# Expert weights in transfers of four tiles with 64 KB rows and of two tiles with 32 KB rows

## Chip, cores and metric

The kernel runs on 1 core of one Trainium2 chip. The metric is the device time of one execution in microseconds (us); lower is better. All numbers are fp32 in memory.

## The reference

Three blocks follow each other on 512 tokens of width 1024. The change touches the last part of the first block, an expert-choice feed-forward layer with 16 experts; each expert picks 64 tokens:

```python
def expert_choice_ffn(h, w_router, w_gate, w_up, w_down):
    Bn, N, D = h.shape                                   # 1, 512, 1024
    cap = max(1, CAPACITY_FACTOR * N // N_EXPERTS)       # 64
    logits = jnp.einsum('bnd,de->bne', h, w_router, preferred_element_type=jnp.float32)
    aff = jax.nn.softmax(logits, axis=-1)
    top_w, top_idx = lax.top_k(jnp.swapaxes(aff, 1, 2), cap)
    xe = jax.vmap(lambda hb, ib: hb[ib])(h, top_idx)
    g = jnp.einsum('becd,edf->becf', xe, w_gate)         # 1024 -> 2048
    u = jnp.einsum('becd,edf->becf', xe, w_up)
    y = jnp.einsum('becf,efd->becd', jax.nn.silu(g) * u, w_down)
    y = y * top_w[..., None].astype(y.dtype)
    return jax.vmap(lambda ib, yb: jnp.zeros((N, D), yb.dtype).at[ib.reshape(-1)].add(yb.reshape(-1, D)))(top_idx, y)
```

Its weights are 16 x 3 x 1024 x 2048 numbers, 403 MB, each used once.

## The kernel before

**Weights as tiles.** All matrices of weights are cut into tiles of 128 partitions x 4096 numbers (16 KB per partition, 2 MB). `Core.tiles` lists them in the order of their use; the expert weights are 192 of them, 12 for each expert: two of gate and two of up for the first half of the 2048 hidden channels, the same for the second half, then four of down. In DRAM the tensor `in_w_exp` holds them as 192 blocks of [128 partitions, 4096], laid out by the host (`expert_tiles`), so a row of one transfer is 16 KB long on both sides.

**Places.** A tile lands in a place in SBUF. The ring has four places (`SLOTS`). In the expert stage four of the seven slabs, buffers of 128 x 4224 numbers for activations that are free there, are four more places (`MORE_SLOTS` = slabs 6, 4, 5, 1). `lay_slots` (L289) gives each tile its place: the first 96 expert tiles (`WIDE_RING`, 8 experts) go round all eight places, the other 96 round the four of the ring. `self.before` remembers the tile that had the place last. Slab 3 holds, in the expert stage, the gathered tokens `xe`, the hidden values `hT` and the results `y`; slab 3 also serves the router for its squares.

**Order of the transfers.** SyncE (SP) issues all weight transfers in the order of the tiles, in `issue_weights` (L314). Before each it waits until TensorE has used the tile that was in the place:

```python
engine.wait_ge(self.weight_used.sem, self.before[n] + 1)
to = self.ring_tile(n)[:, 0:kc, 0:cw] if kc <= KC else self.deep_tile(n, kc)
engine.dma_start(to, src).then_inc(self.weight_in[self.slot[n]].sem, 16)
```

TensorE waits for the landing of each tile with `weight_ready` and raises `weight_used` by one after its last matmul on it. Before the stage, `expert_weights` (a function of the stage for gates, projections and output) issues eight expert tiles ahead: two when the layer `pa` has used its last tile, more after `pb`, the last after `wo`.

**TensorE in the expert stage** (`experts`). Two experts are a pair; expert e has tiles 12e to 12e + 11. A tile is 16 matmuls of 512 columns (`two_halves`, L2335). Between them stand, for even experts after their fourth tile, the combine of the pair before (`combine`, L2325, 16 matmuls), for odd ones at the same place the gather of the next pair's tokens (`gather`, L2264, 64 matmuls), and for all the transposes of the hidden values (`turn`, L2362) and, once per pair, those of the one-hot weights (`turn_onehot`, L2273). The last 8 tiles, numbers 184 to 191, are the down weights of experts 14 and 15 by columns (`last_narrow`, L2290), so that the combine of the last pair (L2303) and the sums for the norm that follows (L2314) stand between them. ScalarE and VectorE move the PSUM results on. After the stage, the next weights (`in_w_in` of the second block) take the places of the ring as they come free.

Of the kernel before, what the change touches and what calls it, by code (L numbers as in the profile page):

```python
# [21 lines left out]
P = 128  # L22
D = 1024
KC = D // P
SEQ = 512
# [3 lines left out]
SLOTS = 4  # L29
SLOT_COLS = 512  # L30
BANKS = 8
EXPERTS, CAP, DFF = 16, 64, 2048
EXPERT_TILES = 12
MORE_SLOTS, WIDE_RING = (6, 4, 5, 1), 8 * EXPERT_TILES
LB = 64
NBLK = 9
WIDE = NBLK * LB
# [3 lines left out]
def common_constants():  # L41

    p = np.arange(P)
    ident = np.eye(P)
    ones = np.ones((P, P))
    head = (p[:, None] // 64 == p[None] // 64)
    four = np.arange(4)[None]
    return [("ident", ident), ("ones", ones), ("head", head),
            ("eye64", p[:, None] % 64 == p[None, :64]), ("first32", p[:, None] % 32 == 0), ("pick16", p[:, None] % 32 == np.arange(16)[None]), ("pick4", p[:, None] == 32 * four),
            ("halves32", p[:, None] // 64 == p[None, :32] // 16), ("pick8", p[:, None] == 16 * p[None, :8])]  # L50
# [114 lines left out]
class Core:  # L165


    def __init__(self, nc, ctx, dram):
        self.nc, self.dram = nc, dram
        sb = lambda name, shape, dt=F32: ctx.enter_context(nc.sbuf_tensor(name, shape, dt))  # L170
        self.ring = [sb(f"ring{i}", [P, KC, SLOT_COLS]) for i in range(SLOTS)]
        self.slab_cols = KC * TOK2
        self.slabs = sb("slabs", [P, 7 * self.slab_cols])
        self.slab = [self.slabs[:, i * self.slab_cols:(i + 1) * self.slab_cols] for i in range(7)]
# [15 lines left out]
        def count(name):  # L190
            s = Count(ctx.enter_context(nc.semaphore(name)))
            self.counts.append(s)
            return s
# [25 lines left out]
        turn = [count(f"of_this_stage{i}") for i in range(37)]  # L219
# [6 lines left out]
                            "plain_read", "held", "rows", "step", "ada", "scaled"))  # L226
        self.deep = named(("product", "first", "second", "third", "fourth", "sums", "read", "step"), 20)

        self.weight_in = [count(f"weight_in_slot{i}") for i in range(SLOTS)] + turn[37 - len(MORE_SLOTS):]
        self.ring += [self.slab[i][:, 0:KC * SLOT_COLS].rearrange("p (k c) -> p k c", k=KC) for i in MORE_SLOTS]  # L230
        self.weight_used = count("weight_used")
        self.tiles, self.named, self.issued, self.done = [], {}, 0, 0
        self.dense = set()
# [50 lines left out]
    def plan_laid_out(self, name, w, i):  # L284

        self.named[name] = [(0, SLOT_COLS, [(len(self.tiles), 0, KC, SLOT_COLS)])]
        self.tiles.append((w[i].rearrange("p (k c) -> p k c", k=KC), KC, SLOT_COLS))

    def lay_slots(self, expert_tiles):  # L289

        slots, first = SLOTS + len(MORE_SLOTS), expert_tiles[0]
        freed = [*range(SLOTS, slots), *((first + i) % (SLOTS - 1) for i in range(SLOTS - 1)), SLOTS - 1]
        self.slot, self.turn, self.before, last, turns = [], [], [], {}, [0] * slots
        for n in range(len(self.tiles)):
            at = n - expert_tiles[0]
            slot = (freed[at % slots] if at < WIDE_RING else at % SLOTS) if n in expert_tiles else n if n < SLOTS else n % (SLOTS - 1)
            self.slot.append(slot)
            self.turn.append(turns[slot])
            self.before.append(last.get(slot))
            last[slot] = n  # L300
            turns[slot] += 1

    def issue_weights(self, engine, upto):

        limit = len(self.tiles) if self.weight_limit is None else self.weight_limit
        while self.issued < limit:
            n = self.issued
            src, kc, cw = self.tiles[n]
            if self.before[n] is not None:
                if self.before[n] >= upto:  # L310
                    break
                engine.wait_ge(self.weight_used.sem, self.before[n] + 1)
            to = self.ring_tile(n)[:, 0:kc, 0:cw] if kc <= KC else self.deep_tile(n, kc)
            engine.dma_start(to, src).then_inc(self.weight_in[self.slot[n]].sem, 16)  # L314
            self.issued += 1

    def deep_tile(self, n, kc):
        return self.ring_tile(n)[:, :, :].rearrange("p k c -> p (k c)").rearrange("p (k c) -> p k c", k=kc)
# [4 lines left out]
        return self.ring[self.slot[n]]  # L323

    def weight_ready(self, engine, n):
        landed = self.weight_in[self.slot[n]]
        engine.wait_ge(landed.sem, landed.at(16 * (self.turn[n] + 1)))

    @contextmanager
    def stage(self):  # L330
# [1372 lines left out]
def first_block(core):  # L1703
    nc, dram = core.nc, core.dram
    X, H, S2, S3, S4, S5, S6 = [s[:, :].rearrange("p (k t) -> p k t", k=KC) for s in core.slab]
    x, h = X[:, :, META:], H[:, :, 0:SEQ]
    flat = [s[:, :] for s in core.slab]
# [163 lines left out]
    for i in range(2):  # L1871
        to = lambda p, i=i: two(u, 2 * i + p)
# [7 lines left out]
    places = [flat[5][:, 2048:3072]], [flat[6][:, 2048:2048 + 2 * D]]  # L1880
# [15 lines left out]
    parts, at, steps = [], {}, 0  # L1896
# [47 lines left out]
              [core.work[:, 0:1024], flat[3][:, 3072:4096]], 64, base=P, rest=[core.work[:, 1024:1408], core.work[:, 1408:1792]])  # L1944


    squares = S3[:, :, 0:SEQ]
    raw = [core.work[:, 1024 * i:1024 * (i + 1)].rearrange("p (k t) -> p k t", k=2) for i in range(2)]
    both = lambda t, p: t[:, 2 * p:2 * p + 2, :]
    act_of = lambda t: lambda k, a, b: t[:, 4 * k:4 * k + 4, a:b]  # L1950
# [17 lines left out]
    places = [core.area[:, 1024 * i:1024 * i + 1024] for i in range(2)]  # L1968
# [9 lines left out]
    pa = SevenProducts(core, "pa", act_of(u), SEQ, flat[4], Carve(places[0]), to_raw, gated, "dve", plain=False)  # L1978
# [15 lines left out]
    def expert_weights(sp):  # L1994

        for layer, tiles in ((pa, 2), (pb, 4 + SLOTS - 1), (wo, 4 + SLOTS)):
            sp.wait_ge(core.weight_used.sem, layer.last_tile + 1)
            core.weight_limit = core.expert_tile + tiles
            core.issue_weights(sp, core.done)
    stage.transfers = expert_weights  # L2000
    stage.run()
    experts(core, x, router.xtok, router.rank, router.aff, core.c("first", "iota"), gain, shift)


# [200 lines left out]
def experts(core, x, xtok, rank, aff, iota, gain, shift):  # L2205
# [3 lines left out]
    flat = [s[:, :] for s in core.slab]  # L2209
# [2 lines left out]
    onehot, weighted = by_tokens(core.area[:, 1024:1536]), by_tokens(core.area[:, 1536:2048])  # L2212
    spread = [core.work[:, 512 + 512 * i:1024 + 512 * i] for i in range(2)]
    sg, hid = core.work[:, 1536:2048], core.work[:, 0:512]
    xe = [flat[3][:, D * i:D * i + D].rearrange("p (k s) -> p k s", k=KC) for i in range(2)]
    hT = flat[3][:, 2 * D:3 * D].rearrange("p (f s) -> p f s", s=CAP)
    y = flat[3][:, 3 * D:4 * D]
    G, U, T, Y = core.bank[0:4]
    XB, CB = core.bank[4:6], core.bank[6:8]
    last_y, last_comb = (Y, T), (*CB, *XB)  # L2220
# [9 lines left out]
                (core.use_params("p2", columns([(n, np.zeros((1, w))) for n, w in PARAMS["p1"]])[1]), core.dram["p2"]),  # L2230
                (core.area[:, 0:columns(masks)[1]], core.dram["second"])]
    for landed, slot in zip(core.weight_in[SLOTS:], range(SLOTS, len(core.weight_in))):
        landed.add(16 * core.slot.count(slot))
    core.weight_limit = core.rwkv_limit
    squares = core.slab[6].rearrange("p (k t) -> p k t", k=KC)[:, :, 0:SEQ]
    with core.stage() as block:
# [2396 lines left out]
def plan_rest(core):  # L4633
    plan_second(core)
    plan_third(core)
# [6 lines left out]
def program(nc, dram, out):  # L4642
    with ExitStack() as ctx:
        ctx.enter_context(nc.allow_non_contiguous_dma("parameters and tiles"))
        core = Core(nc, ctx, dram)
        core.place("common", common_constants(), core.common)
        w_in = dram["w_in"]
        halves = lambda name, w, c: [(f"{name}{i}", w, c + 512 * i, c + 512 * i + 512) for i in range(2)]
        kv = [("kv", w_in, 3 * D, 3 * D + 512)]
        for i in range(4):  # L4650
            core.plan_laid_out(f"ada{i}", dram["w_ada"], i)
        core.plan(*kv[0])
        for i, tile in enumerate([*halves("va", w_in, D), *halves("q", w_in, 2 * D), *halves("u", w_in, 0), None, None]):
            core.plan_laid_out(f"ada{4 + i}", dram["w_ada"], 4 + i)
            if tile:
                core.plan(*tile)
        core.plan("ga", w_in, 3 * D + 512, 4 * D + 512)
        core.plan("gb", w_in, 4 * D + 512, 5 * D + 512)
        core.plan("pa", dram["w_proj_a"], 0, D)
        core.plan("pb", dram["w_proj_b"], 0, D)  # L4660
        core.plan("wo", dram["w_out"], 0, D)
        core.expert_tile = len(core.tiles)
        for n in range(EXPERTS * EXPERT_TILES):
            core.tiles.append((dram["w_exp"][n].rearrange("p (k c) -> p k c", k=KC), KC, SLOT_COLS))
        plan_rest(core)
        core.lay_slots(range(core.expert_tile, core.expert_tile + EXPERTS * EXPERT_TILES))
        if "rwkv_v" in core.named:

            core.rwkv_limit = core.named["rwkv_v"][-1][2][-1][0] + 1
        first_block(core)  # L4670
        on_x = second_block(core)
        third_block(core, out, on_x)


def expert_tiles(x):

    wide = lambda w: w.reshape(EXPERTS, 2, 4, P, 2, D).transpose(0, 4, 1, 3, 2, 5)
    gate, up = wide(x["w_exp_gate"][0]), wide(x["w_exp_up"][0])
    down = x["w_exp_down"][0].reshape(EXPERTS, 4, 4, P, D).transpose(0, 1, 3, 2, 4)
    tiles = np.concatenate([gate[:, 0], up[:, 0], gate[:, 1], up[:, 1], down], 1)  # L4680
    tiles = np.ascontiguousarray(tiles).reshape(EXPERTS * EXPERT_TILES, P, 4 * D)
    by_columns = x["w_exp_down"][0][-2:].reshape(2, 2, KC, P, 2, 512).transpose(4, 0, 1, 3, 2, 5)
    tiles[-16:-8] = tiles[-12:-4].copy()
    tiles[-8:] = by_columns.reshape(8, P, 4 * D)
    return tiles


def laid_out(inputs):
# [31 lines left out]
```

## Time and profile before

| | us |
|---|---|
| median of 3 runs | 3627.23 (3621.87 to 3627.24) |
| the profiled execution | 3625.37 |
| its span, first to last instruction | 3623.6 |
| TensorE busy | 3395.9 (94%) |
| VectorE busy | 1449.0 (40%) |
| ScalarE busy | 703.0 (19%) |
| weights and activations moved | 602.01 MB, mean 166 GB/s |

The span has a long tail of small stages behind the expert stage; the expert stage lies between about 667 and 1599 us. The page divides the span in 40 slices of 90.6 us. The share of TensorE's busy time says little there: matmuls are pipelined and their ends are modelled. The columns of windows and of the timeline are named in the section on the rows; PEclk is the TensorE clock that was granted, DMA share is the mean busy share of the core's 16 DMA engines.

### The profile page before, as it was taken

The page shows a single profiled execution, that of the slowest core. Times are in us where ns is not written, and L with a number is a line of the kernel's source. Part 1 is how long each engine was busy: PE and PEld are TensorE (multiplying, and loading weights), DVE is VectorE, ACT ScalarE, POOL GpSimd, SP SyncE. Part 2 cuts the span into 40 slices and gives each one's busy share as a digit, 9 for nine tenths or more (in the row PEclk, how much of TensorE's full clock was granted, in tenths as well). Part 3 has the DMA queues.
Part 4 walks back from the last instruction along what each step waited for, and adds up shares of the span by engine and source line. Part 5 has one row for each costly group of instructions (what it writes and reads, how often), then busy time and mean ns, then how long its engine had stood idle before and what let it go on. Part 6 is the DMA issues. An engine that isn't in the chain of part 4 may idle for free. (4 is left out here: it accounts for less than half of the span.)

```text
span 3623.6 us, 56784 instructions
## 1 busy us (share of the span) xinstructions
PE 3395.9 (94%) x24513; PEld 2412.8 (67%) x24513; DVE 1449.0 (40%) x3086; ACT 703.0 (19%) x1553; POOL 192.5 (5%) x261
## 2 busy tenths in 40 slices
PE   8999999998888888889988899999999999999998
PEld 5877888433332333257777777788888888888666
DVE  2476455211011101123655454645532646544344
ACT  2127310200000000012454115212100101101232
POOL 0000000000000000000355000300000000000000
PEclk9999999999999999999999999999999999999999
DMA  6540124699999999970000220222222321221120
GB/s 243 193 151 27 44 74 186 267 428 428 428 427 426 426 425 426 427 286 24 3 4 16 89 62 27 97 70 90 74 93 70 104 83 47 94 77 61 52 72 24
DMA packets 130168, 602.01 MB, mean 166 GB/s; under 512 B 8160, under 2 KB 38624, under 8 KB 103424
## 3 DMA queue, kind: packets, MB, share of 16 engines
q1 hardware_dynamic: 125600, 589.94, 41.0%
q10 hardware_dynamic: 4320, 8.44, 1.0%
q8 instruction: 195, 3.19, 0.4%
q14 instruction: 53, 0.43, 0.0%
HBM read 587.82 MB, written 2.10 MB: 163 GB/s over the span
## 5 line engine op out<-in xcount | busy, mean ns | idle before, releaser
L3086 PE MATMUL banks<-slabs,ring 128*128 128x256 f32 (+1 forms) x4456 | 1002.8, 383 | 14.7 <-DVE ring L3232 5.4
L3086 PEld LDWEIGHTS banks<-slabs,ring 128*128 128x128 f32 x4456 | 841.7, 190 | 152.7 <-issue 29.3
L2335 PE MATMUL banks<-ring,slabs 128*64 128x512 f32 x2176 | 489.2, 598 | 75.4 <-DMA ring<-in_w_exp 68.8
L2335 PEld LDWEIGHTS banks<-ring,slabs 128*64 128x64 f32 x2176 | 154.4, 137 | 390.5 <-issue 305.4
L3086 PE MATMUL banks<-ring 128*128 128x256 f32 (+1 forms) x920 | 215.1, 382 | 4.1 <-DVE ring L3227 3.4
L2506 DVE TENSOR_TENSOR work<-work,banks 128x512 f32<-128x512 f32 x32 | 22.0, 687 | 488.1 <-PE banks L2335 471.4
L401 PE MATMUL banks<-slabs,ring 128*128 128x264 f32 (+3 forms) x712 | 196.1, 432 | 3.2 <-PEq L331 1.9
L3086 PEld LDWEIGHTS banks<-ring 128*128 128x128 f32 x920 | 173.2, 190 | 33.0 <-issue 8.7
L2335 PE MATMUL banks<-slabs 128*64 128x512 f32 x768 | 171.3, 595 | 17.5 <-DMA slabs<-in_w_exp 14.6
L3434 PE MATMUL banks<-slabs,ring 128*128 128x264 f32 x768 | 172.4, 386 | 1.6 <-issue 1.6
L401 PEld LDWEIGHTS banks<-slabs,ring 128*128 128x128 f32 (+1 forms) x712 | 131.1, 188 | 59.7 <-issue 35.7
L3434 PEld LDWEIGHTS banks<-slabs,ring 128*128 128x128 f32 x768 | 145.8, 190 | 26.8 <-issue 1.9
L2335 PEld LDWEIGHTS banks<-slabs 128*64 128x64 f32 x768 | 54.0, 137 | 124.7 <-issue 101.9
L3190 ACT COPY slabs<-banks 128x256 f32<-128x256 f32 (+2 forms) x71 | 27.5, 388 | 545.9 <-PE banks L3086 504.1
L3227 DVE TENSOR_TENSOR ring<-ring 128x512 f32<-128x512 f32 (+1 forms) x93 | 68.0, 731 | 152.5 <-PE banks L3086 134.7
L2434 ACT ACTIVATE work<-banks 128x512 f32<-128x512 f32 x32 | 19.1, 597 | 524.3 <-PE banks L2335 524.3
L1442 ACT ACTIVATE slabs<-slabs,small 128x513 f32<-128x513 f32 (+7 forms) x136 | 97.1, 714 | 89.1 <-DVE small L1398 89.0
L2513 DVE COPY slabs<-banks 64x512 f32<-64x512 f32 x28 | 19.3, 689 | 226.3 <-PE banks L2335 226.1
L1313 PE MATMUL banks<-slabs 64*128 64x256 f32 (+10 forms) x544 | 98.5, 443 | 7.9 <-DVE small L1394 4.1
L3230 DVE TENSOR_TENSOR ring<-ring 128x512 f32<-128x512 f32 (+1 forms) x93 | 68.1, 732 | 87.5 <-PE banks L3086 76.9
L3232 DVE TENSOR_TENSOR ring<-ring 128x512 f32<-128x512 f32 (+1 forms) x93 | 68.0, 732 | 84.3 <-PE banks L3086 76.0
L3797 POOL MEMSET ring<- 128x48 f32 x2 | 0.3, 138 | 1676.8 <-PE banks L401 1671.4
(635 smaller groups left out, 4418.8 us busy)
## 6 DMA issues: line engine op xcount, KB each, us to landing
ring<-in_w_exp SPq DMA_DIRECT2D x144, 2048.0 KB, 15.8
slabs<-in_w_exp SPq DMA_DIRECT2D x48, 2048.0 KB, 32.6
ring<-in_w_in SPq DMA_DIRECT2D x19, 2048.0 KB, 11.8
ring<-in_w_ff SPq DMA_DIRECT2D x16, 2048.0 KB, 8.3
ring<-in_even_w_in SPq DMA_DIRECT2D x14, 2048.0 KB, 8.7
ring<-in_w_ada SPq DMA_DIRECT2D x12, 2048.0 KB, 10.6
ring<-in_w_out SPq DMA_DIRECT2D x4, 2048.0 KB, 7.8
ring<-in_even_w_out SPq DMA_DIRECT2D x4, 2048.0 KB, 8.3
```

Of the source, the lines that this page charges most:

```text
L401: mm = core.nc.tensor.matmul(to, lhsT, rhs, start=kk0 + k < g, stop=kk0 + k >= kcs - g)
L1313: mm = nc.tensor.matmul(score[h][0:m, at:at + cols], *products[j], start=j == 0, stop=j == count - 1)
L1442: nc.scalar.activation(r, r, ACT.Exp, bias=st[0:m, h:h + 1], scale=scale, accum_out=st[0:m, 2 + h:3 + h]).then_inc(e_ready.sem, e_ready.ad ...
L2335: ins = mm(out[64 * c:64 * c + CAP, :], lhsT[:, k, :], w[:, at:at + 512], start=first and k == 0, stop=last and k == 3)
L2506: nc.vector.tensor_tensor(hid, sg, U[:, :], ALU.mult).then_inc(moe["hidden"].sem, moe["hidden"].add(1))
L2513: ins = nc.vector.tensor_copy(y[64 * s:64 * s + CAP, 512 * half:512 * half + 512], Y[64 * half:64 * half + CAP, :])
L3086: last = mm(bank, a[:, k, :], b[:, k, :], start=k == 0, stop=k == h - 1)
L3190: self.done(nc.scalar.copy(self.to(p, 1, 0), self.bank[p, 4]), "held")
L3227: self.done(tt(A[1][1], A[1][1], A[1][0], ALU.subtract), "second")
L3230: self.done(tt(A[0][0], A[1][1], A[0][0], ALU.add), "first")
L3232: self.done(tt(A[0][1], A[0][1], A[1][1], ALU.subtract), "fourth")
L3434: last = mm(self.bank(which), a[:, k, :], self.fourth(t, k) if which == 4 else b[:, k, :], start=t == 0 and k == 0, stop=t == 1 and k == 7)
```

## The change

- In DRAM four tiles that follow each other lie side by side: `in_w_exp` is now [48, 128 partitions, 16384], so a row of up to four tiles is contiguous, 64 KB.
- The ring is one buffer, and the four more places lie side by side in slabs 3 to 6 (`places`, from the start of slab 3, 4 x 4096 numbers). The expert stage's `xe`, `hT` and `y` move from slab 3 to slab 1, and the router's squares from slab 3 to slab 1 (`H`).
- `lay_slots` marks tiles that go together. From expert tile 8 to tile 175, a round of eight is one transfer of four tiles into the slabs (64 KB rows) and two transfers of two tiles into the ring (32 KB rows). Of the first eight, tiles 0 and 1 and tiles 2 and 3 are pairs into the slabs and the rest are single. The last 16 tiles go singly round the four places of the ring, as the last 96 did.
- A transfer of several tiles waits until the last of all the tiles that had its places is used (`max(before)`), and raises one semaphore, on which each of its tiles waits.
- The first expert tiles also wait for the last pair of `pa` (`pair_done`), which reads slab 3.

```diff
-MORE_SLOTS, WIDE_RING = (6, 4, 5, 1), 8 * EXPERT_TILES
+MORE_SLOTS, MORE_FROM, WIDE_RING = 4, 3, 22 * 8
...
-        self.ring = [sb(f"ring{i}", [P, KC, SLOT_COLS]) for i in range(SLOTS)]
+        self.in_ring = sb("ring", [P, SLOTS * KC * SLOT_COLS])
...
+    def places(self, slot, n):
+
+        size = KC * SLOT_COLS
+        if slot < SLOTS:
+            return self.in_ring[:, slot * size:(slot + n) * size]
+        at = MORE_FROM * self.slab_cols + (slot - SLOTS) * size
+        return self.slabs[:, at:at + n * size]
+
...
+            in_turn = freed if at < slots else [*range(SLOTS, slots), *range(SLOTS)]
+            slot = (in_turn[at % slots] if at < WIDE_RING else at % SLOTS) if n in expert_tiles else n if n < SLOTS else n % (SLOTS - 1)
             self.slot.append(slot)
-            self.turn.append(turns[slot])
             self.before.append(last.get(slot))
             last[slot] = n
-            turns[slot] += 1
+            count = 4 if slots <= at and slot >= SLOTS else 2
+            if n in expert_tiles and at < WIDE_RING and at % count and slot == self.slot[n - 1] + 1 and slot % count:
+                self.together[n - at % count] = count
+                self.landing.append(self.landing[n - 1])
+            else:
+                self.landings[slot] += 1
+                self.landing.append((slot, self.landings[slot]))
...
-            if self.before[n] is not None:
-                if self.before[n] >= upto:
+            count = self.together.get(n, 1)
+            before = [b for b in self.before[n:n + count] if b is not None]
+            if before:
+                if max(before) >= upto:
                     break
-                engine.wait_ge(self.weight_used.sem, self.before[n] + 1)
-            to = self.ring_tile(n)[:, 0:kc, 0:cw] if kc <= KC else self.deep_tile(n, kc)
+                engine.wait_ge(self.weight_used.sem, max(before) + 1)
+            if count > 1:
+                at = n - self.expert_tile
+                to, src = self.places(self.slot[n], count), self.dram["w_exp"][at // 4, :, at % 4 * KC * SLOT_COLS:(at % 4 + count) * KC * SLOT_COLS]
+            else:
+                to = self.ring_tile(n)[:, 0:kc, 0:cw] if kc <= KC else self.deep_tile(n, kc)
             engine.dma_start(to, src).then_inc(self.weight_in[self.slot[n]].sem, 16)
-            self.issued += 1
+            self.issued += count
...
-    squares = S3[:, :, 0:SEQ]
+    squares = H[:, :, 0:SEQ]
...
             sp.wait_ge(core.weight_used.sem, layer.last_tile + 1)
+            if layer is pa:
+                pa.pair_done(sp, 3)
             core.weight_limit = core.expert_tile + tiles
...
-    xe = [flat[3][:, D * i:D * i + D].rearrange("p (k s) -> p k s", k=KC) for i in range(2)]
-    hT = flat[3][:, 2 * D:3 * D].rearrange("p (f s) -> p f s", s=CAP)
-    y = flat[3][:, 3 * D:4 * D]
+    xe = [flat[1][:, D * i:D * i + D].rearrange("p (k s) -> p k s", k=KC) for i in range(2)]
+    hT = flat[1][:, 2 * D:3 * D].rearrange("p (f s) -> p f s", s=CAP)
+    y = flat[1][:, 3 * D:4 * D]
```

How the order on SP changes. First the start of the expert stage: before, the issues behind the three small loads.

```order
L2240 DMA slabs<-in_meta 128x8x16
L2240 DMA param<-in_p 128x94
L2240 DMA area<-in_second 128x1024
L314 DMA slabs<-in_w_exp 128x4096 [waits weight_used] x4
L314 DMA ring<-in_w_exp 128x4096 [waits weight_used] x4
L314 DMA slabs<-in_w_exp 128x4096 [waits weight_used] x4
```

The same place now; a shape is partitions x numbers per partition.

```order
L2264 DMA slabs<-in_meta 128x8x16
L2264 DMA param<-in_p 128x94
L2264 DMA area<-in_second 128x1024
L335 DMA slabs<-in_w_exp 128x16384 [waits weight_used]
L335 DMA ring<-in_w_exp 128x8192 [waits weight_used] x2
L335 DMA slabs<-in_w_exp 128x16384 [waits weight_used]
```

Where four issues each waited for their own tile, one now waits for the last of four; a round of eight issues is a round of three.

The second place is the end of the rounds of eight. Before, it stands at tile 96, where the long row of single transfers into the ring begins:

```order
L314 DMA ring<-in_w_exp 128x4096 [waits weight_used] x4
L314 DMA slabs<-in_w_exp 128x4096 [waits weight_used] x4
L314 DMA ring<-in_w_exp 128x4096 [waits weight_used] x100
```

Now it stands at tile 176:

```order
L335 DMA slabs<-in_w_exp 128x16384 [waits weight_used]
L335 DMA ring<-in_w_exp 128x8192 [waits weight_used] x2
L335 DMA ring<-in_w_exp 128x4096 [waits weight_used] x16
```

The rounds with the slabs go on for 80 tiles more, and single transfers are left for the last 16 tiles. The order of the instructions on TensorE in the expert stage is the same.

## Rows read from the trace of the kernel before

**Rows 1.** The page: busy tenths of PE and DMA, and GB/s, in 40 slices.

```profile
PE   8999999998888888889988899999999999999998
...
DMA  6540124699999999970000220222222321221120
GB/s 243 193 151 27 44 74 186 267 428 428 428 427 426 426 425 426 427 286 24 3 4 16 89 62 27 97 70 90 74 93 70 104 83 47 94 77 61 52 72 24
```

**Rows 2.** Windows of the expert stage; header line names the columns.

```profile
core 0: us, PE busy (x) PEld busy (x) DVE busy (x) ACT busy (x) POOL busy (x), PEclk, DMA share, GB/s
680.00:1587.00 907.00, 809.04 (x3878) 309.96 (x3878) 106.65 (x170) 56.97 (x109) 0.00 (x0) 1.00 1.00 426
800.00:1140.00 340.00, 297.46 (x1402) 112.28 (x1398) 37.98 (x60) 18.89 (x37) 0.00 (x0) 1.00 1.01 428
```

**Rows 3.** Waits between 725 and 1570 us: waiting line, releaser, total us, times, longest.

```profile
PE banks L2335 <- DMA ring<-in_w_exp: 68.8, 55, 2.5
...
PE banks L2335 <- DMA slabs<-in_w_exp: 14.6, 12, 1.3
```

**Rows 4.** The page's DMA issues: KB each, median us to landing.

```profile
ring<-in_w_exp SPq DMA_DIRECT2D x144, 2048.0 KB, 15.8
slabs<-in_w_exp SPq DMA_DIRECT2D x48, 2048.0 KB, 32.6
```

**Rows 5.** Timeline of PE, 1464 to 1535 us: start, duration, instruction, idle before.

```profile
1492.66 7.89 PE L2325 MATMUL banks<-work,slabs 128*128 128x512 f32 x16
1500.48 7.09 PE L2335 MATMUL banks<-ring,slabs 128*64 128x512 f32 x32
...
1523.40 3.65 PE L2335 MATMUL banks<-ring,slabs 128*64 128x512 f32 x16 [1.33 <-DMA ring<-in_w_exp]
1528.21 3.65 PE L2335 MATMUL banks<-ring,slabs 128*64 128x512 f32 x16 [1.16 <-DMA ring<-in_w_exp]
```

**Rows 6.** Timeline of SP's DMA issues, 560 to 760 us.

```profile
568.30 24.57 SPq L314 DMA_DIRECT2D slabs<-in_w_exp  x4
592.91 50.74 SPq L314 DMA_DIRECT2D ring<-in_w_exp  x4
...
677.84 10.63 SPq L314 DMA_DIRECT2D slabs<-in_w_exp  x4
```

**Rows 7.** Windows inside two loads of dense weights (2 KB rows).

```profile
449.50:453.50 4.00, 4.00 (x20) 3.54 (x19) 1.12 (x2) 0.37 (x1) 0.00 (x0) 1.00 1.05 402
498.00:502.00 4.00, 4.00 (x21) 3.51 (x20) 1.12 (x2) 0.37 (x1) 0.00 (x0) 1.00 1.04 398
```

**Rows 8.** Line L314, the issues between 670 and 690 us.

```profile
L314 SPq DMA_DIRECT2D slabs<-in_w_exp x4: 327/328/328, 677.8 to 688.1; - x4
...
DMA to landing us min/median/max: 7.6/9.8/13.0
```

**Rows 9.** Timeline of PE, 666 to 760 us.

```profile
674.14 13.95 PE L2335 MATMUL banks<-slabs 128*64 128x512 f32 x64
...
695.92 7.09 PE L2335 MATMUL banks<-ring,slabs 128*64 128x512 f32 x32
...
718.05 13.90 PE L2335 MATMUL banks<-ring,slabs 128*64 128x512 f32 x64
731.88 7.41 PE L2264 MATMUL banks<-area,slabs 128*128 128x128 f32 x64
...
746.24 0.66 PE L2362 MATMUL banks<-common,work 128*128 128x128 f32 x4
746.74 0.60 PE L2273 MATMUL banks<-common,area 128*128 128x128 f32 x4
```

**Rows 10.** Timeline of SP's DMA issues, 1500 to 1512 us.

```profile
1504.18 7.93 SPq L314 DMA_DIRECT2D ring<-in_w_exp  x3
```

**Rows 11.** Timelines of PE and SP, 1570 to 1600 us.

```profile
1588.11 3.67 PE L2290 MATMUL banks<-ring,slabs 128*64 128x256 f32 x32
...
1586.37 3.56 SPq L314 DMA_DIRECT2D ring<-in_w_in  x3
```

More of the change, by code:

```diff
@@ L227, in __init__ @@
         self.deep = named(("product", "first", "second", "third", "fourth", "sums", "read", "step"), 20)
-        self.weight_in = [count(f"weight_in_slot{i}") for i in range(SLOTS)] + turn[37 - len(MORE_SLOTS):]
-        self.ring += [self.slab[i][:, 0:KC * SLOT_COLS].rearrange("p (k c) -> p k c", k=KC) for i in MORE_SLOTS]
+        self.weight_in = [count(f"weight_in_slot{i}") for i in range(SLOTS)] + turn[37 - MORE_SLOTS:]
+        self.ring = [self.places(i, 1).rearrange("p (k c) -> p k c", k=KC) for i in range(SLOTS + MORE_SLOTS)]
         self.weight_used = count("weight_used")
@@ L287, in plan_laid_out @@
         self.tiles.append((w[i].rearrange("p (k c) -> p k c", k=KC), KC, SLOT_COLS))
+    def places(self, slot, n):
[4 more added lines that the diff above has]
+        return self.slabs[:, at:at + n * size]
     def lay_slots(self, expert_tiles):
-        slots, first = SLOTS + len(MORE_SLOTS), expert_tiles[0]
+        slots, first = SLOTS + MORE_SLOTS, expert_tiles[0]
         freed = [*range(SLOTS, slots), *((first + i) % (SLOTS - 1) for i in range(SLOTS - 1)), SLOTS - 1]
-        self.slot, self.turn, self.before, last, turns = [], [], [], {}, [0] * slots
+        self.slot, self.landing, self.before, last, self.landings = [], [], [], {}, [0] * slots
+        self.together = {}
         for n in range(len(self.tiles)):
             at = n - expert_tiles[0]
-            slot = (freed[at % slots] if at < WIDE_RING else at % SLOTS) if n in expert_tiles else n if n < SLOTS else n % (SLOTS - 1)
+            in_turn = freed if at < slots else [*range(SLOTS, slots), *range(SLOTS)]
+            slot = (in_turn[at % slots] if at < WIDE_RING else at % SLOTS) if n in expert_tiles else n if n < SLOTS else n % (SLOTS - 1)
             self.slot.append(slot)
-            self.turn.append(turns[slot])
             self.before.append(last.get(slot))
             last[slot] = n
-            turns[slot] += 1
+            count = 4 if slots <= at and slot >= SLOTS else 2
[5 more added lines that the diff above has]
+                self.landing.append((slot, self.landings[slot]))
     def issue_weights(self, engine, upto):
@@ L325, in weight_ready @@
     def weight_ready(self, engine, n):
-        landed = self.weight_in[self.slot[n]]
-        engine.wait_ge(landed.sem, landed.at(16 * (self.turn[n] + 1)))
+        slot, turn = self.landing[n]
+        landed = self.weight_in[slot]
+        engine.wait_ge(landed.sem, landed.at(16 * turn))
     @contextmanager
@@ L2232, in experts @@
     for landed, slot in zip(core.weight_in[SLOTS:], range(SLOTS, len(core.weight_in))):
-        landed.add(16 * core.slot.count(slot))
+        landed.add(16 * core.landings[slot])
     core.weight_limit = core.rwkv_limit
@@ L4663, in program @@
         for n in range(EXPERTS * EXPERT_TILES):
-            core.tiles.append((dram["w_exp"][n].rearrange("p (k c) -> p k c", k=KC), KC, SLOT_COLS))
+            core.tiles.append((dram["w_exp"][n // 4].rearrange("p (i k c) -> p i k c", i=4, k=KC)[:, n % 4], KC, SLOT_COLS))
         plan_rest(core)
@@ L4684, in expert_tiles @@
     tiles[-8:] = by_columns.reshape(8, P, 4 * D)
-    return tiles
+    return np.ascontiguousarray(tiles.reshape(-1, 4, P, 4 * D).transpose(0, 2, 1, 3)).reshape(-1, P, 16 * D)
 def laid_out(inputs):
```

## Prediction

> **What bounds the kernel now.** I read the page first. Over the span TensorE is busy for 94%, but in slices 10 to 17 its digit is 8 while the DMA digit is 9 and the rate stands flat at 425 to 428 GB/s [rows 1]. Those slices are the 16 experts. The windows say it more sharply: from 680 to 1587 us the DMA engines are busy 1.00 of the time and move 426 GB/s, while TensorE is busy 809 of 907 us, at clock 1.00 [rows 2]. The waits between 725 and 1570 us name the releaser: the expert matmuls (L2335) start late behind DMAs 67 times, 83 us in all [rows 3]. So the stage ends when its last weights have landed. 192 tiles of 2048 KB [rows 4] come in one unbroken stream; TensorE has slack in each tile (a run of 16 matmuls takes 3.65 us and then waits 1.2 to 1.3 us [rows 5]). Time is won here only by a faster stream, an earlier start of it, or fewer holes in it.
>
> A tile takes 2.097 MB / 428 GB/s = 4.90 us in the stream. I number the expert tiles 0 to 191. Tiles 0 to 7 are prefetched before the stage; tile 8 opens the stream. Its issue is the first of a row of four that begins at 677.84 us, paced by TensorE (10.63 us from the first to the end of the fourth) [rows 6].
>
> **Part 1: longer rows.** A tile moves 16 KB per partition, so each of 16 engines handles 8 rows per tile. With the change, tiles 8 to 175 (21 rounds of 8) move as one transfer of four tiles with 64 KB rows and two of two tiles with 32 KB rows: 2 and 4 rows per tile and engine. The price of a row comes from the same trace. Loads of dense weights have 2 KB rows, 64 per engine in 2048 KB; inside such loads the rate is 402 and 398 GB/s [rows 7], 400 in the mean, so 2.097 MB take 5.24 us. The step to 4.90 us removed 56 rows per engine: 0.34 / 56 = 6.1 ns per row. So a tile in a slab saves 6 rows or 0.037 us, one in the ring 4 rows or 0.024 us; 84 tiles of each kind: 3.1 + 2.0 = **5.1 us less**. Ends: 0, if the rows are cut back to 16 KB on the way; 168 x 8 x 6.1 ns = 8.2 us, if the cost of rows vanishes. I take 5.1, since the measured step extrapolates straight to it. The order shows 85 transfers in place of 192. This is worth nothing by itself, because in the stream nothing waits between transfers: one landing alone needs 7.6 us [rows 8], in the stream 4.9.
>
> The Trainium skill (DMA: Bandwidth & Descriptors, Bandwidth) puts a DMA at a fixed 2.0 us plus its bytes over 436 GB/s. By that rule 2 MB would take 6.8 us and 107 transfers fewer would save 214 us. The rows above disagree: the fixed part is hidden behind the transfer ahead in the queue.
>
> **Part 2: the stream starts later.** Before, tile 8 is issued as soon as tile 0 is used. Now tiles 8 to 11 are one transfer, which waits for tile 3. SP issued tile 11 at 677.84 + 10.63 - 0.33 = 688.14 us [rows 6], so the stream opens 688.14 - 677.84 = **10.3 us later**. All 8 prefetched tiles are there, so nothing is queued meanwhile, and no later point gives it back: a stream without holes shifts as a whole. The ring pairs of 12 to 15 wait for tiles 6 and 7, used by 703.0 us [rows 9], long before this transfer of four ends (about 710 us).
>
> **Part 3: holes in the middle.** A slab transfer can be issued when its four old tiles are used. Let one land at T. The two ring pairs behind it take 4 x 4.87 = 19.5 us, so the next slab transfer must be ready to stream by T + 19.5. TensorE uses the four by T + 3.65 + 3 x 3.46 = T + 14.0 (3.46 is a quarter of the 13.8 us between starts of the run of 64 at 718.05 and the next at 731.88 [rows 9]), plus 1.2 us at most for the transposes between them (L2362, L2273: 0.5 and 0.7 us [rows 9]). An issue needs 7.6 - 4.9 = 2.7 us before it streams [rows 8]. That makes T + 17.9: a margin of 1.6 us, **no hole**. The combine (7.9 us) falls between a slab transfer's tiles and the ring tiles behind them: the pair that landed at T + 9.7 is used by T + 14.0 + 7.8 + 6.9 = T + 28.7 and wanted again at T + 39. The gather (7.4 us [rows 9]) falls where TensorE waits for a slab transfer.
>
> **Part 4: the change-over at tile 176.** Before, eight places are used up to tile 95 and four (the ring) from tile 96; now eight up to 175. Tiles 168 to 171, the first of expert 14, land at T as one transfer. The stream then holds 172 to 175 until T + 19.5, and next comes tile 176, alone, in the place of 172. TensorE: T + 14.0, then the combine of the pair before, 7.8 us (1492.66 to 1500.48 [rows 5]), then tile 172, 3.5 us: used at T + 25.3. The issue lands 7.6 us later, at T + 32.9, where an unbroken stream would have T + 24.4: **8.5 us of hole**. Before, the same combine stood beside singly landed tiles: tile 176 was issued at 1504.18 us [rows 10] and there was no hole (the expert tiles behind it still came 4.8 us apart [rows 5]).
>
> **Part 5: the rest.** The first tiles are issued behind one wait more (the last pair of the layer pa, which frees slab 3). What is queued behind it on SP are later expert tiles only. Before, tiles 0 to 3 went out from 568.3 to 592.9 and the last of the eight at 643.6 us, 30 us before their first use at 674.14 [rows 6, 9]: a few us cost nothing. If that cover were gone, the start of the stage would wait for the landing. Operands moved between slabs (xe, hT, y, squares) keep shape and engine: nothing.
>
> **Sum**: -5.1 + 10.3 + 8.5 = +13.7 us. At the end every microsecond counts: the last expert matmuls stand right behind the last tile (L2290 at 1588.11, 3.67 us [rows 11]), and the next weights (L314, in_w_in at 1586.37) follow the used places. The profiled execution took 3625.4 us; I forecast **3639 us**. The median of the runs shown is 3627.2, 1.9 us above it.
>
> **The rivals.**
> - *The rows are cut to 16 KB on the way* (the change does not do what it says to the stream). Gain 0: 3625.4 + 18.8 = 3644. Nothing in the trace excludes it. Chance 0.08.
> - *The gain covers the cost.* All of the row cost goes (8.2 us), and so do the small pauses: 426 GB/s over the whole stream against 428 in its first part is 4 us. 18.8 - 12.2 = +6.6: 3632, no change that can be measured. For it: pauses may belong to transfers. Against: they would all have to go. Chance 0.20.
> - *Faster: long rows raise the rate itself.* From 2 to 16 KB, three doublings, the rate rose 7%, 2.3% per doubling. If that went on, 64 KB rows gain 4.7% and 32 KB rows 2.3%, 3.5% of 168 x 4.90 = 823 us: 29 us, net -10: 3615. It decides from 26 us saved, which is 442 GB/s. Against: the cost per row is a constant and small, and the DMA engines are already busy 1.00. Chance 0.08.
> - *The margin of part 3 is not there.* If an 8 MB transfer needed 4.7 us instead of 2.7 to stream, the 14 of 21 slab transfers with transposes between their tiles would each open some 0.5 us of hole, and part 2 would grow by 2 us: +9 more, 3648. Chance 0.08.
> - *Long rows are slower to read.* Rows that start 64 KB apart could collide in HBM. As bound, the rate of the 2 KB rows: 168 x (5.24 - 4.90) = 57 us instead of -5: 3701. Chance 0.03. The Trainium skill (DMA: Bandwidth & Descriptors, Latency and other measured facts) reports HBM copies losing speed at row pitches of large powers of two, little at 512 KiB and half from 4 MiB; no row here has such a pitch.
> - *A fixed cost per transfer is in the stream after all*: 107 x 2.7 = 289 us faster, 3350. The rows speak against it. Chance 0.01.
>
> **How the numbers follow.** My forecast has 0.52; inside it the gain lies between 0 and 8.2 and the two delays within 3 us. A measurement of this kernel can tell about 0.2%, 7.3 us, from no change. Slower by more: 0.52 + 0.08 + 0.08 + 0.03 = 0.71. Same: 0.20. Faster: 0.09. The range from 3628 to 3652 takes in the forecast, the cut rows, the covered cost and the lost margin, and leaves out the cases at 3615, 3350 and 3701.
>
> **What would show it.** In the profile after: transfers of 8192 KB and 4096 KB on SP; the first inside the stage near 688 us, not 678; a DMA rate of 430 to 431 GB/s between 750 and 1480 us; TensorE waiting longer but less often for DMAs (once for each transfer, up to 5 us); a slice with a lower DMA digit near 1510 us and tile 176 issued some 25 us after the landing of tile 168; the stage's end near 1612 in place of 1598 us. I am wrong if the rate passes 436, if holes show in each round, or if the dip near 1510 us is missing.

## The result: slower by 1%, and the profile after

The changed kernel took 3665.78 us (median of 4 runs, 3658.71 to 3669.89) against 3626.11 us before (4 runs): ratio 1.0104, 95% interval 1.0091 to 1.0117, some 40 us more. I had forecast 3639 us and at most 3652. The direction was right, the size was three times too small. In three of the experiments (pairs, single transfers, one wait) one execution fell into a slower state, which the ratios leave out; in the last two it was the one with the trace, so nothing is read from those traces.

The page of the changed kernel, the same lines as in [rows 1] and the granted clock, with slices of 91.7 us:

```profile
PE   8999999888988898889988899999999999999998
...
PEclk9999999999999999999999999999999999999999
DMA  6540124699999999880000220212222221221220
GB/s 251 181 163 11 47 91 162 259 421 410 424 405 424 417 418 427 368 367 23 2 4 11 82 73 27 73 69 92 92 69 92 90 94 47 92 69 58 61 72 24
```

The plateau is no longer flat: 405 to 427 GB/s where [rows 1] had 425 to 428, though rows are longer. The same stretch of both kernels as a window, first before, then after (the columns are those of [rows 2]):

```profile
750.00:1490.00 740.00, 654.05 (x3048) 243.97 (x3046) 87.05 (x135) 41.30 (x80) 0.00 (x0) 1.00 1.01 427
```

```profile
750.00:1490.00 740.00, 652.59 (x2972) 252.39 (x2974) 85.01 (x132) 41.80 (x81) 0.00 (x0) 0.94 0.98 418
```

Two things changed there: the DMA share fell from 1.01 to 0.98, and the granted clock of TensorE fell from 1.00 to 0.94. The waits between 725 and 1600 us (compare [rows 3]) name mostly one releaser, the transfers into the slabs:

```profile
PE banks L2359 <- DMA slabs<-in_w_exp: 88.7, 20, 9.9
...
PE banks L2359 <- DMA ring<-in_w_exp: 5.5, 6, 1.2
```

TensorE waits about as long in all as before (94 us against 83), but 89 us of it in 20 waits for slab transfers, of up to 9.9 us, where there were 67 waits of at most 2.5 us.

**Where the time went.** The stretch from the first small load of the expert stage (`in_meta`, SP) to the first load of the next stage (`in_gate_w`) grew from 933.7 to 971.2 us, by 37.5 us. The part in front of it is 0.5 us shorter, the scan stage behind it took 420.9 instead of 414.5 us, and the rest of the program 1.0 us more. The 37.5 us, by the issues and landings in the trace (a step is the time from one landing to the next: the pair issued at 982.13 us landed at 1012.89, the transfer of four issued at 1009.13 landed at 1033.55, a step of 20.7 us):

| term | forecast | measured |
|---|---|---|
| the stream opens later | +10.3 | +10.3 |
| hole at the change-over, tile 176 | +8.5 | +11.7 |
| 20 slab transfers behind the first, over 19.35 us each | 0 | +23.0 |
| longer rows | -5.1 | -8.2 |
| sum | +13.7 | +36.8 |

The last 0.7 us are in small pauses of the stream. The 7.4 us behind the stage are in no theory below; their cause stays open.

### The profile page after: what moved, and what is told of

It is laid out like the page before. It is cut to its first block and busy times, and to the rows that moved or that the text cites. A ratio compares the mean times of both kernels' runs of the same rounds, so it can differ in the third digit from the quotient of the medians.

```text
span 3668.1 us, 56678 instructions
## 1 busy us (share of the span) xinstructions
PE 3420.0 (93%) x24513; PEld 2436.6 (66%) x24513; DVE 1450.3 (40%) x3086; ACT 702.7 (19%) x1553; POOL 192.5 (5%) x261
## 3 DMA queue, kind: packets, MB, share of 16 engines
q8 instruction: 195, 3.19, 0.4%
## 5 line engine op out<-in xcount | busy, mean ns | idle before, releaser
L2359 PE MATMUL banks<-slabs 128*64 128x512 f32 x1408 | 340.9, 643 | 101.5 <-DMA slabs<-in_w_exp 96.8
L2359 PE MATMUL banks<-ring,slabs 128*64 128x512 f32 x1536 | 338.3, 594 | 10.2 <-DMA ring<-in_w_exp 5.5
L2359 PEld LDWEIGHTS banks<-slabs 128*64 128x64 f32 x1408 | 114.6, 148 | 312.7 <-issue 306.2
L2359 PEld LDWEIGHTS banks<-ring,slabs 128*64 128x64 f32 x1536 | 108.6, 137 | 225.0 <-issue 212.5
```

What stands on the lines that cost most here:

```text
L2359: ins = mm(out[64 * c:64 * c + CAP, :], lhsT[:, k, :], w[:, at:at + 512], start=first and k == 0, stop=last and k == 3)
```

## The theories

Theory C, the clock: a transfer of four lands as a whole, so TensorE stands idle for up to 10 us ahead of it; its granted clock halves, the four tiles are then used up to 3 us more slowly, the next transfer of four is issued too late, and the stream has a hole. Theory S: a transfer of four needs more time from its issue to the stream than I had put in, and the clock only follows. Theory L: the new layout in DRAM or the new places read more slowly.

The timeline of TensorE in the changed kernel, around three transfers of four:

```profile
792.00 15.60 PE L2359 MATMUL banks<-slabs 128*64 128x512 f32 x64 [8.93 <-DMA slabs<-in_w_exp]
...
831.94 7.09 PE L2359 MATMUL banks<-slabs 128*64 128x512 f32 x32 [1.90 <-DMA slabs<-in_w_exp]
...
1033.68 15.93 PE L2359 MATMUL banks<-slabs 128*64 128x512 f32 x64 [9.38 <-DMA slabs<-in_w_exp]
```

After a wait of 1.90 us two tiles (32 matmuls) take 7.09 us, as before; after 8.93 and 9.38 us four tiles take 15.60 and 15.93 us, where [rows 9] have 13.90 and 13.95 us. Shorter waits do it too, though not each time: in this trace the first two tiles took 8.7 to 9.5 us behind the eight waits of 2.3 to 4.2 us and 7.09 us behind the five of at most 1.9 us; in the second run of the same kernel they also took 7.09 us behind waits of 2.50 and 2.74 us. The windows around the last row show the clock (third column from the end):

```profile
1024.00:1032.00 8.00, 0.30 (x2) 0.00 (x0) 1.38 (x2) 0.00 (x0) 0.00 (x0) 0.72 0.90 389
1032.00:1037.00 5.00, 3.32 (x8) 1.12 (x10) 0.00 (x0) 0.00 (x0) 0.00 (x0) 0.50 0.99 426
1037.00:1044.00 7.00, 7.00 (x34) 2.58 (x32) 0.00 (x0) 0.60 (x1) 0.00 (x0) 0.95 1.01 435
```

It falls while TensorE is idle and stands at 0.50 (1.2 of 2.4 GHz) when the tiles have landed. The Trainium skill (TensorE: Matmul & The Clock Gate, HAM oscillation) describes just this: a wait for a DMA ahead of each tile throttles the array again, so that each tile starts cold. The trace agrees: clock 0.94 over the stretch, and runs of four tiles 12 to 22% longer behind waits of 7 to 10 us (15.52 to 16.93 us). I had not weighed that rule.

The kernel before has no such waits (at most 2.5 us [rows 3]) and clock 1.00 [rows 2].

## The experiments

**Pairs instead of fours.** Layout, places and change-over as in the change.

```diff
-            count = 4 if slots <= at and slot >= SLOTS else 2
+            count = 2
```

> All transfers of a round are of two tiles (32 KB rows), in the slabs too; the layout in DRAM, the places and the change-over at tile 176 stay. Theory C (clock): TensorE's waits for a transfer of four (7 to 9 us) halve its granted clock just after, the four tiles are used 2 to 3 us later and the next transfer of four comes too late. Then pairs, with waits of 3 to 4 us at most, bring the dips of the clock and the holes down to almost none, tile 8 starts 3.4 us later than before instead of 10.3, the hole at tile 176 shrinks to about 2 us, and rows of 32 KB save 6.5 us: 3622 to 3628 us, no change that can be measured against before. Theory L (the new layout or the places read more slowly): 3645 us or more, with steps of over 9.8 us per pair.

3626.08 us, ratio 0.9994 (0.9984 to 1.0003): 3622 to 3628 was theory C's answer. The stage took 935.0 us, the rate between 750 and 1490 us is 431 GB/s with DMA share 1.00. So the slowdown sits in the transfers of four. The clock still dipped in places (0.97 in that window, runs of two tiles of up to 9.8 instead of 7.09 us), which theory C had hardly expected; it cost nothing here, as there was time to spare.

**Single transfers in the new layout.** `count = 1` at the same place.

> Every expert tile is a transfer of its own again (rows of 16 KB, now 64 KB apart in DRAM), with eight places up to tile 175. Theory C: waits as in the kernel before, clock 0.99, a step of 4.89 us per tile, 3626 us within 3. Theory L: slower steps, over 4.95 us per tile, 3636 us or more.

3627.77 us, ratio 0.9997 (0.9987 to 1.0007). The layout and the places cost nothing that the time shows; theory L falls.

**Extra matmuls in the waits.** In `two_halves`, ahead of the first tile of a transfer of four:

```diff
+                if core.together.get(n) == 4:
+                    for i in range(24):
+                        mm(out[64 * (i % 2):64 * (i % 2) + CAP, :], lhsT[:, 0, :], xtok[:, 0, 0:512], start=True, stop=True)
```

> The changed kernel with 24 more matmuls of 512 columns (5.2 us, results overwritten) ahead of the first tile of each transfer of four, so that TensorE is idle 2 to 4 us there instead of 7 to 9. Transfers, rows and waits of SP are the same. Theory C: the granted clock stays 1.00 in the expert stage, the four tiles are used in 14 us instead of 16 to 17, the slab steps fall from 20.5 to about 19.5 us: 15 to 25 us off, 3641 to 3651 us. Theory S (a transfer of four starts late by itself, the clock only follows): the holes stay, 3660 us or more.

3753.5 us, ratio 1.0345 (1.0327 to 1.0362): a miss of my own making. Each call is two matmul instructions in the trace, so that the 24 calls take 10.4 us and not 5.2, longer than the waits. Still one thing can be read: there was no dip of the clock in the whole stage, and runs of 64 took 13.9 us again.

**Shorter extra matmuls.** `range(4 if (n - n0) % 24 == 16 else 12)`.

> As the run before with extra matmuls, which turned out to be two instructions each (48 instead of 24, 10.4 us, longer than the wait they stood in). Now 12 calls (24 instructions, 5.2 us) ahead of a transfer of four, and 4 calls (1.7 us) where the gather stands ahead of it. Theory C: no dips of the clock in the expert stage, runs of 64 matmuls in 13.9 us, slab steps of about 19.5 to 20 us instead of 20.5: the stage 10 to 20 us shorter than in the change, 3645 to 3655 us. Theory S (a transfer of four starts late by itself): steps of 20.5 us remain, 3663 us or more.

3666.1 us, ratio 1.0106 (1.0088 to 1.0123): by the time alone theory S. But the trace shows two faults. Behind 5.3 us of extra work the long waits still left TensorE idle for 3.1 to 4.3 us, and the clock still fell; and where the wait was short (after the combine) the extra work itself delayed the tiles, by 2.6 us in the rows below (the transfer had landed at 833.55 us) and by up to 5.2 us in other rounds:

```profile
793.10 15.65 PE L2362 MATMUL banks<-slabs 128*64 128x512 f32 x64 [4.30 <-DMA slabs<-in_w_exp]
...
831.02 5.32 PE L2356 MATMUL banks<-slabs 128*64 128x512 f32 x24
836.17 7.04 PE L2362 MATMUL banks<-slabs 128*64 128x512 f32 x32
```

So this run decides nothing by its time. Its transfers of four, taken one by one, say more: where one was issued 4.2 us or more ahead of the landing before it, its step was 19.35 us in five of six cases; at 0.2 us after that landing, 23.2 us. That gave the measure for the next attempt.

**Extra matmuls fitted to the waits.** `range(18 if (n - n0) % 24 == 0 else 16 if n - n0 == 8 else 4)`.

> Extra matmuls fitted to the waits as the changed kernel shows them: 7.8 us ahead of the slab tiles that open an even expert (waits of 7 to 10 us), 6.9 us ahead of tile 8, 1.7 us ahead of the others (waits of 1 to 4 us), so that they fill the waits and delay little. In the traces so far a step of a transfer of four grows once it is issued less than about 4.2 us ahead of the end of the stream; at full clock the four are used early enough for 4.2 to 4.7 us. Theory C: no dips of the clock in the stage, leads of 4.2 us and more, sum of the holes in the rounds halved at least (from about 20 us to under 10), 3650 to 3656 us. Theory S: the lead is too short at full clock too, holes as before, 3662 us or more.

3645.86 us, ratio 1.0052 (1.0034 to 1.0069): 16 to 20 us less than the change (3662.0 and 3665.8 us in its two runs), and less than the 3650 to 3656 expected, with more work on TensorE and the same transfers. The stage took 953.9 us, 17.3 less. The window and the same round as above:

```profile
750.00:1490.00 740.00, 711.00 (x3362) 264.78 (x3360) 85.88 (x134) 42.35 (x82) 0.00 (x0) 1.00 1.00 427
```

```profile
1017.72 7.89 PE L2356 MATMUL banks<-slabs 128*64 128x512 f32 x36
1026.94 13.95 PE L2362 MATMUL banks<-slabs 128*64 128x512 f32 x64 [1.33 <-DMA slabs<-in_w_exp]
```

Clock 1.00, four tiles in 13.95 instead of 15.93 us (so in six of the seven transfers of four that are used in one run of 64; one took 15.65 us, behind a wait of 1.97 us). I call lead the time by which a transfer of four is issued before the landing ahead of it. Its mean over the 20 transfers rose from 3.19 to 4.57 us, and the sum of what the steps take over 19.35 us fell from 23.0 to 7.3 us (the second run of the change has 3.17 and 21.0 us). Theory C is shown as the cause of most of the holes. The 7.3 us that are left fit theory S, but that is argued and not shown, and the lead alone does not sort them: at full clock steps of 20.2 and 20.3 us stand at leads of 3.90 and 5.37 us, steps of 19.37 us at 3.89 and 5.37 us too.

**One wait, two landings.** Pairs, but the first slab pair waits for the last of four old tiles.

```diff
+            four = 4 if 8 <= at < WIDE_RING and self.slot[n] >= SLOTS and at % 4 == 0 else count
-            before = [b for b in self.before[n:n + count] if b is not None]
+            before = [b for b in self.before[n:n + four] if b is not None]
```

> As the run with pairs, but the pair for the first two slab places waits until all four old tiles are used, as the transfer of four does: late issue as in the change, landing in halves as with pairs. Theory C: the wait of TensorE is what costs, and it is short here; no dips, no holes in the rounds; only the late start stays (10.3 us) and most of the hole at tile 176: about 3632 us. If the late issue itself makes the holes: 3650 us or more.

3637.41 us, ratio 1.0023 (1.0013 to 1.0033), nearer to the 3632 expected than to the 3650 of the other case. The same kernel once more, for its trace:

> A second look at the kernel in which a slab round is two pairs that both wait for the last of four old tiles, for its trace. Issue times in the rounds as in the change or earlier; TensorE's waits for slab tiles under 4 us; steps of 9.7 us per pair, no holes in the rounds; time about 3637 us as measured.

```profile
PE banks L2361 <- DMA ring<-in_w_exp: 39.8, 23, 4.1
PE banks L2361 <- DMA slabs<-in_w_exp: 39.0, 20, 2.6
```

3632.14 us in that one run. The waits are 4.1 us at most, the first pair of a round is issued 7.5 to 13.6 us ahead of the landing before it, and no round has a hole. In the rounds, waiting for four old tiles is harmless; waiting for four new ones is not. At the opening it still has its price: the stage took 940.5 us, with free pairs 935.0. The clock dipped here too (0.97), which cost nothing. This run changes the leads as well as the clock, so it is the fitted matmuls, and not this run, that tell theory C from theory S.

**The change-over one round later.** `WIDE_RING = 23 * 8`.

> The changed kernel with one round of eight more (WIDE_RING = 23 * 8): the change-over moves from tile 176, where a combine stands between the slab tiles and the ring tiles, to tile 184, where none does. If the hole at the change-over (tile 176 lands 16.6 us after tile 175) is that combine: 8 us off, about 3657 us. If it comes from going from eight places to four as such: no change, 3665 us.

3656.16 us, ratio 1.0077 (1.0064 to 1.0091): 6 to 10 us less; the stage 962.5 us. The first single tile lands 7.2 us behind the transfer ahead, not 16.6. The hole is the combine, as forecast. In the changed kernel it reads:

```profile
1514.22 16.30 PE L2359 MATMUL banks<-slabs 128*64 128x512 f32 x64 [7.89 <-DMA slabs<-in_w_exp]
1530.44 7.90 PE L2349 MATMUL banks<-work,slabs 128*128 128x512 f32 x16
1538.27 7.09 PE L2359 MATMUL banks<-ring,slabs 128*64 128x512 f32 x32
```

```profile
1541.96 27.21 SPq L335 DMA_DIRECT2D ring<-in_w_exp  x8
```

```profile
1534.00:1545.00 11.00, 11.00 (x41) 3.41 (x40) 4.08 (x6) 0.00 (x0) 0.00 (x0) 1.00 0.21 69
```

Four tiles, combine, one tile, then SP's issue (27.9 us after the landing; I had 25.3), and meanwhile a DMA share of 0.21.

**The first round in single transfers.** Tiles 8 to 15 singly, fours from tile 16.

> The changed kernel, but with tiles 8 to 15 (the first round inside the stage) in single transfers, so that tile 8 is issued as soon as tile 0 is used. The stream opens at 678 us as before. If the late opening costs its full 10 us: 3655 us. If it is absorbed by the later waits: 3665 us.

3651.06 us, ratio 1.0063 (1.0045 to 1.0081): 11 to 15 us less, a little more than the 10 expected; the stage 958.8 us, 12.4 less than in the change and 10 less than in its second run. The first issue comes 13.4 us behind the first small load, not 22.1 and 23.6 as in those two, and the holes behind transfers of four sum to 18.5 us, not 23.0 and 21.0. The late opening costs about its full price.

**The change once more.**

> The changed kernel once more, on this chip. The expert stage should again be 37 us longer than before (it depends on waits and lengths that repeat). The 6 us more in the scan stage behind it, if they are only where the dips of the clock happen to fall, should change from profile to profile: between 412 and 421 us for that stage. If they belong to the change, 421 us again.

3662.02 us, ratio 1.0097 (1.0082 to 1.0111); the stage 968.7 us, the scan stage 422.5 us. Over the traces that are read here that stage took 411 to 415 us, except 418 to 423 us in the four with unfilled long waits and 420 us in the first run with extra matmuls, which has no dip of the clock in the expert stage. The instructions there are the same. "421 us again" was the answer for a cost that belongs to the change; what makes it is not shown, and its cause stays open.

**Best with pairs.** Pairs, tiles 8 to 15 singly, change-over at 184.

> Pairs everywhere (32 KB rows), the first round inside the stage in single transfers so that the stream opens as early as before (678 us), and the change-over at tile 184. Theory C: no start delay, no hole, short waits; rows of 32 KB save 0.038 us a tile: 6 us, 3620 us, 0.9983 of before. If waits for pairs still cost by their dips of the clock, only 3 us or less are won: 0.999 to 1.000.

3623.02 us, ratio 0.9988 (0.9980 to 0.9997); the stage 927.6 us, 6.1 less than before. The gain of the stage is about the 6 us forecast for the rows; in the time it is 0.1%, little above the noise. Between 750 and 1490 us the rate is 431 GB/s, the clock 0.97.

**All three costs taken out of the fours.**

Fitted extra matmuls, tiles 8 to 15 singly, change-over at 184.

> The changed kernel with all three costs taken out at once, transfers of four kept: fitted extra matmuls in the waits (-20 us alone), the first round inside the stage in single transfers (-13 us alone), the change-over at tile 184 (-8 us alone). If the three are separate and add up, 3665 - 20 - 13 - 8 = 3624 us, back at the kernel before, with the gain of the longer rows (about 8 us) eaten by what is left of the holes. If they overlap, 3630 us or more.

3628.07 us, ratio 0.9998 (0.9989 to 1.0007), the stage 935.4 us against 933.7 before. The three parts account for the slowdown, within 4 us of the sum (3624 us). Its transfers of four still have 11.4 us of holes; the gain of the longer rows covers most of them.

## Why the prediction was wrong

- **Part 1, longer rows**: right, mis-sized. Unbroken, a step is 9.70 to 9.71 us for a pair and 19.35 us for four, against 2 x 4.894 and 4 x 4.894 us: 0.041 and 0.056 us per tile, 8.2 us in all where the sum had 5.1. That it meets my upper end (8 rows per tile at 6.1 ns) is chance: what went are 4 and 6 rows per tile, at 9 to 10 ns each. The windows of 2 KB rows underpriced a row. In the trace before, a packet of 2 KB took 84 ns (the median between 440 and 560 us), so 64 of them 5.38 us where the windows had given 5.24; that would have made (5.38 - 4.89) / 56 = 8.6 ns. The formula with a fixed 2.0 us, which the prediction takes from the Trainium skill, stands there in DMA: Bandwidth & Descriptors under Anatomy of one DMA, as a fit to transfers that GpSimd issues; nothing in the sum rests on it. A stretch of the change with few holes (1376 to 1470 us), and before:

```profile
DMA packets 976, 40.68 MB, mean 433 GB/s; under 512 B 97, under 2 KB 97, under 8 KB 97
```

```profile
DMA packets 2753, 40.13 MB, mean 427 GB/s; under 512 B 304, under 2 KB 304, under 8 KB 304
```

- **Part 2, the opening**: right. First issue at 687.66 us, in a stage that began 0.47 us earlier: 10.3 us, and nothing gave it back.
- **Part 3, "no hole"**: this step failed, and it is the 23 us that the sum of the stage lacks (what parts 1 and 4 missed cancels, by luck: -3.1 and +3.2 us). It set T + 3.65 + 3 x 3.46 for the use of four tiles, a price from a stretch in which TensorE had never been idle for more than 2.5 us. The change itself made the waits of 7 to 10 us, where I had put "up to 5 us" without a sum, and with them half the clock: 15.5 to 16.9 us for four tiles in place of 14.0. An estimate from the same rows was at hand: a round is 8 x 4.85 = 38.8 us, its eight tiles and the transposes take some 30 us, which leaves about 9 us where no combine or gather fills it. The step also set 2.7 us from issue to stream, from a single tile; for four tiles the first issue shows

```profile
DMA to landing us min/median/max: 22.9/22.9/22.9
```

  22.9 - 19.35 = 3.5 us. Also, of the parts that the 16 DMA engines carry of a transfer of four, the last landed 0.6 to 3.1 us behind the first, so the engines do not end together, which may be why even leads of 3.5 to 4.2 us were too short: 16 of the 19 transfers of the change with a lead under 4.2 us took over 19.5 us. The slower clock alone takes 1.5 to 2.9 us, as much as the margin or more; with the matmuls that kept it up, 7.3 of the 23.0 us stayed.
- **Part 4, the change-over**: right in place and mechanism, 11.7 instead of 8.5 us. 2.3 us are the clock (16.30 instead of 14.0 us for the four), 0.9 us the issue (8.5 us to the landing instead of 7.6). With the fitted matmuls tile 176 was issued 25.4 us after the landing, as forecast, and the hole was 8.3 us.
- **Part 5**: right. The first pair was issued at 568.33 us as before, and the part ahead of the stage did not grow.
- **The rivals**: "the margin of part 3 is not there" was the right place, with the chance of 0.08 and +9 us; its reason was half of the truth. The rates of the cut rows, of the faster and of the slower rows did not come: packets are longer, and the stream runs at 431 to 433 GB/s where it is unbroken. Nor did the small pauses go: before, a step of 6.2 us in place of 4.9 stands at 928, 1174 and 1420 us; with pairs (the best kernel), one of 11.3 us in place of 9.7 at 936, 1180 and 1425 us.

## What to carry to other kernels

When a change makes landings larger, price what the consumer does after the longer wait, not only whether the queue stays full: at about equal total waiting, a few long waits cost TensorE its clock, and the late release comes back as a hole in the stream. Give a margin of a few microseconds a second look with each of its terms taken under the new conditions. A larger transfer can wait for all its old tiles at once if it lands in parts; check the first round and each change of the scheme, where one large transfer has nothing ahead of it in the queue to hide behind.

## What was not expected of the hardware

- The gain per row did not level off: from 16 to 64 KB it followed a nearly constant cost of 9 to 10 ns per row and engine (16 KB rows: 4.894 us per tile; 64 KB rows: 4.838 us).
- A transfer of 8 MB with nothing ahead of it needs 3.5 us more than its time in the stream, one of 2 MB 2.7 us [rows 8].
- The stream pauses for 1.3 to 1.6 us about every 245 us, with transfers of one tile and of two alike (the steps above).
- Extra matmuls that nobody reads made the changed kernel 16 to 20 us faster, because the tiles behind the waits were then used at full clock.
